# Gate and up projections as 2x2 block products with seven products, in a one-core decoder step

## What is computed

```
def rmsnorm(x, g, eps=RMS_EPS):
    xf = x.astype(jnp.float32)
    y = xf * lax.rsqrt(jnp.mean(xf * xf, axis=-1, keepdims=True) + eps)
    return (y * g.astype(jnp.float32)).astype(x.dtype)

def swiglu(h, w_gate, w_up, w_down):
    return (jax.nn.silu(h @ w_gate) * (h @ w_up)) @ w_down
...
# x += 0.5 * swiglu(rmsnorm(x)), D_MODEL = 1024, D_FF = 2816
# 512 prompt tokens and 64 sample tokens: T = 576 in all
```

## Time and profile before

| | us |
|---|---|
| median of three runs | 3361.85 (3356.53 to 3365.54) |
| the profiled execution, its own time | 3364.43 |
| its span, first to last instruction | 3362.6 |
| PE busy | 3111.3 (93%) |
| DVE busy | 1586.9 (47%) |
| ACT busy | 1170.0 (35%) |
| POOL busy | 424.7 (13%) |
| mean granted TensorE clock | 0.965 |

### The profile page before, as it was taken

The page is one execution under the profiler, slowest core; times in us unless marked ns, Lnnn a source line. Parts: engine busy times, 40 slices in busy tenths (PEclk is TensorE's granted clock), DMA queues, the critical chain, the costliest instruction groups (busy, mean ns, idle before and its releaser), DMA issues.

```text
span 3362.6 us, 70237 instructions
## 1 busy us (share of the span) xinstructions
PE 3111.3 (93%) x29771; PEld 2977.8 (89%) x29771; DVE 1586.9 (47%) x1892; ACT 1170.0 (35%) x1766; POOL 424.7 (13%) x352
## 2 busy tenths in 40 slices
PE   5999996999999988999999999798788997799999
PEld 5999996679999978999999999778788886799999
DVE  4333445556666654433444334444356654544333
ACT  3322223355555532322233222123344543233222
POOL 3000010220000003000020000400144433300000
PEclk9999998999999989999999999899899998899999
DMA  2222222011111102222222222311000001122222
GB/s 107 84 78 88 72 71 71 17 51 32 32 39 52 61 13 76 79 76 96 69 93 75 78 86 72 105 50 63 17 10 11 16 17 38 65 86 72 91 78 75
DMA packets 69248, 206.88 MB, mean 62 GB/s; under 512 B 25346, under 2 KB 42115, under 8 KB 53827
## 3 DMA queue, kind: packets, MB, share of 16 engines
q1 hardware_dynamic: 69058, 204.16, 18.3%
HBM read 198.63 MB, written 5.49 MB: 61 GB/s over the span
## 4 chain that ended last, share of the span: by engine, by line
PE 73%; DVE 6%; ACT 3%; issue 2%; POOL 1%; POOLq 0%; ACTq 0%; DVEq 0%
PE PS L233 45%; PE PS L1074 10%; PE PS L1706 6%; PE PS L1055 1%; PE PS L1101 1%; PE PS L1567 1%; DVE Y L2134 1%; PE PS L707 1%; PE PS L726 1%; PE PS L708 1%; PE PS L245 0%; PE PS L1078 0%; DVE MXP L1180 0%; DVE T L1626 0%; DVE XL L1636 0%
## 5 line engine op out<-in xcount | busy, mean ns | idle before, releaser
L233 PE MATMUL PS<-XH,WH 128*128 128x288 f32 x3520 | 759.2, 297 | 32.2 <-DVE XL L2374 17.7
L233 PE MATMUL PS<-XL,WH 128*128 128x288 f32 x3520 | 754.4, 296 | 0.0
L233 PE MATMUL PS<-XH,WL 128*128 128x288 f32 x3520 | 753.7, 296 | 0.0
L233 PEld LDWEIGHTS PS<-XH,WH 128*128 128x128 f32 x3520 | 569.7, 190 | 38.2 <-DVE WL L219 18.4
L233 PEld LDWEIGHTS PS<-XL,WH 128*128 128x128 f32 x3520 | 569.4, 190 | 0.0
L233 PEld LDWEIGHTS PS<-XH,WL 128*128 128x128 f32 x3520 | 569.1, 190 | 0.0
L219 DVE TENSOR_TENSOR WL<-RAW,WH 128x2048 fp32r<-128x2048 f32 (+1 forms) x184 | 421.6, 2292 | 286.6 <-ACT WH L214 285.7
L214 ACT ACTIVATE WH<-RAW 128x2048 fp32r<-128x2048 f32 (+1 forms) x185 | 344.4, 1862 | 388.4 <-PE PS L233 357.8
L329 ACT ACTIVATE T<-T 128x576 f32<-128x576 f32 x88 | 60.4, 686 | 706.6 <-DVE T L355 706.6
L233 PE MATMUL PS<-HH,WH 128*128 128x288 f32 x1408 | 300.8, 294 | 0.0
L233 PE MATMUL PS<-HH,WL 128*128 128x288 f32 x1408 | 300.0, 294 | 0.0
(11 more groups left out here) (483 smaller groups left out, 4387.0 us busy)
## 6 DMA issues: line engine op xcount, KB each, us to landing
RAW<-in_w SPq DMA_DIRECT2D x113, 1024.0 KB, 4.8
RAW<-in_w SPq DMA_DIRECT2D x32, 768.0 KB, 4.2
RAW<-in_w SPq DMA_DIRECT2D x32, 640.0 KB, 3.9
ROWS<-in_cache_c SPq DMA_DIRECT2D x128, 128.0 KB, 2.0
ROWS<-in_cache_kr SPq DMA_DIRECT2D x128, 32.0 KB, 1.8
RAW<-in_w SPq DMA_DIRECT2D x8, 384.0 KB, 3.2
X<-in_x SPq DMA_DIRECT2D x1, 2304.0 KB, 8.6
out_y<-X SPq DMA_DIRECT2D x1, 2304.0 KB, 6.9
```

Of the source, the lines that this page charges most:

```text
L233: mm = pe.matmul(PS[:, s, 2 * t + half, 0:HT], w[s][:, c:c + P], x[:, k, half * HT:(half + 1) * HT], start=(k == 0 and p == 0), stop=(k == ...
```

## The change

**Seven products.** In each FFN the first two gate-and-up items stay as they are. The other 20 are taken as a 2x2 block product: rows of blocks are gate and up, the inner index is the two halves of the 8 k tiles (k and k + 4), the columns are the two halves of the tokens. Winograd's form of Strassen's product makes of the eight block products seven, each of 4 k tiles x 3 = 12 matmuls of 288 columns: 84 matmuls instead of 96. It wants four sums of weight blocks for each item (S1 to S4, each 128 x 512), four sums of activations once for each FFN (t123_dve, t4_dve and their roundings), and sums of products behind PE.

**Who does what.** S1 is an addition on DVE; S3, S2 and S4 are three subtractions on POOL in a row, each from the one before it. ACT rounds the three own blocks and the four sums, DVE splits them. PE does the products in the order 5, 1, 7, 6, 2, 3, 4. Products 6, 3 and 4 are added onto banks that hold products 1, 5 and 7, so ACT first copies each of these aside (`keep_act` into `KEPT`), and PE waits for the copies. DVE adds up the four results, scales the gate half alone, and leaves the up half unscaled; 1/rms of the up half is put into `HALF` = 0.5/rms, by which down items are scaled.

**Parts and down items.** The 22 tiles are done in four parts of 4, 6, 6 and 6. A down item now holds two output tiles (d and d + 4), so that there are 4 for each part and 16 for each FFN as before, of 48 or 72 matmuls. They are evacuated by two DVE instructions of 1152 elements. The first down item leaves the last hidden row to the end.

**Around the FFN.** `norm_sums` moves behind the first item. Squares are taken on ACT in pairs, and POOL only adds them. FFN 2 and the latent projection take the k tiles in the order 0, 4, 1, 5, ... ACT's, DVE's, SP's and POOL's loops over an FFN are written out; PE keeps a loop over pairs of gate items. In the recurrence several semaphores are counted on one (`kk`, `y_norm`); its instructions stay the same.

```diff
-PARTS = (12, 10)
+PARTS = (4, 6, 6, 6)
...
+    def first_sum_dve(dve, n, js):
+        s = n % 2
+        dve.wait_ge(raw_in[s], 16 * (n // 2 + 1))
+        if n >= 2:
+            dve.wait_ge(multiplied, n - 1)
+        dve.tensor_tensor(sum_place(s, S1, "f"), RAW[s][:, 2 * QB:3 * QB], RAW[s][:, 3 * QB:4 * QB], ALU.add).then_inc(s1_ok, 1)
+
+    def sums_pool(pool, n, js):
+        s = n % 2
+        r = lambda b: RAW[s][:, b * QB:(b + 1) * QB]
+        pool.wait_ge(raw_in[s], 16 * (n // 2 + 1))
+        if n >= 2:
+            pool.wait_ge(multiplied, n - 1)
+        pool.tensor_tensor(sum_place(s, S3, "f"), r(0), r(2), ALU.subtract).then_inc(summed, 1)
+        pool.wait_ge(summed, 3 * js + 1)
+        pool.tensor_tensor(sum_place(s, S2, "f"), r(3), sum_place(s, S3, "f"), ALU.subtract).then_inc(summed, 1)
+        pool.wait_ge(summed, 3 * js + 2)
+        pool.tensor_tensor(sum_place(s, S4, "f"), r(1), sum_place(s, S2, "f"), ALU.subtract).then_inc(summed, 1)
...
+    def gate_pe(pe, n, i, j, ji, f, first=False):
...
+        pe.wait_ge(gate_lo, 5 * j + 3 + ji * 5)
+        pe.wait_ge(evacuated, n - 1 + CREDIT + i)
+        if first:
+            pe.wait_ge(t_split, 4 * f + 4)
+        whole(5).then_inc(part_mm, 1)
+        whole(1).then_inc(part_mm, 1)
+        pe.wait_ge(gate_lo, 5 * j + 4 + ji * 5)
+        whole(7).then_inc(part_mm, 1)
+        pe.wait_ge(gate_lo, 5 * j + 5 + ji * 5)
+        pe.wait_ge(kept, 3 * j + 2 + ji * 3)
+        whole(6, again=True).then_inc(part_mm, 1)
+        whole(2)
+        pe.wait_ge(item_split, n + 1 + i)
+        whole(3, again=True)
+        if first:
+            pe.wait_ge(t4_split, 4 * f + 4)
+        pe.wait_ge(e_ok, j + 1 + ji)
+        whole(4, again=True).then_inc(multiplied, 1)
...
+    def gate_dve(dve, n, js):
...
+        dve.wait_ge(multiplied, n + 1)
+        dve.wait_ge(kept, 3 * js + 3)
+        dve.tensor_tensor(T12[:, 0:HT], PS[:, s, 1, 0:HT], KEPT[:, 1, :], ALU.add)
+        dve.tensor_tensor(c12_21, PS[:, s, 2:4, 0:HT], u2, ALU.add)
+        dve.wait_ge(e_ok, js + 1)
+        dve.tensor_tensor(T12[:, 3 * HT:4 * HT], PS[:, s, 0, 0:HT], M57[:], ALU.add).then_inc(evacuated, 1)
+        dve.wait_ge(evacuated, n + 1 + CREDIT)
+        dve.tensor_tensor(T12[:, 0:T], T12[:, 0:T], RSTD[:], ALU.mult).then_inc(gate_scaled, 1)
...
+        for part, (n, cnt, j, _) in enumerate(hidden_steps(f)):
+            lone = 0
+            js = j - 2 * f - 2
+            if part == 0:
+                multiply_item(pe, n, 0, KD, 2, XH, XL, before=lambda k: pe.wait_ge(xhat_split, base + k + 1), order=order)
+                norm_sums(pe, norm, (n + 1) % 2)
+                pe.wait_ge(root, norm + 1)
+                multiply_item(pe, n + 1, 0, KD, 2, XH, XL)
+                gate_pe(pe, n + 2, 0, js + 2, 0, f, first=True)
+                gate_pe(pe, n + 3, 0, js + 3, 0, f)
+                lone = 4
...
+            for x in range(cnt):
+                plain = part == 0 and x < 2
+                more = x + 1 < cnt and not (part == 0 and x == 0)
                 if more:
-                    split_item(dve, n + u + 1, i)
...
+                    gate_own_act(act, n + x + 1)
+                else:
+                    round_item(act, n + x + 1, cols=ITEM if plain else 2 * cnt * P)
...
+                if not plain:
+                    keep_act(act, n + x, js + x, 0, first=part == 0 and x == 2)
+                if x:
+                    silu_act(act, j + x - 1)
+                if more:
+                    gate_sum_act(act, n + x + 1, js + x + 1, S1)
+                if not plain:
+                    keep_act(act, n + x, js + x, 1, first=part == 0 and x == 2)
+                if more:
+                    gate_sum_act(act, n + x + 1, js + x + 1, S3)
+                    gate_sum_act(act, n + x + 1, js + x + 1, S2)
+                if x:
+                    hidden_act(act, j + x - 1, x - 1)
+                if not plain:
+                    keep_act(act, n + x, js + x, 2, first=part == 0 and x == 2)
+                if more:
+                    gate_sum_act(act, n + x + 1, js + x + 1, S4)
...
+                if x:
+                    scaled(x - 1)
...
+                if more:
+                    first_sum_dve(dve, n + x + 1, js + x + 1)
+                    gate_own_dve(dve, n + x + 1, js + x + 1)
+                    gate_sum_dve(dve, n + x + 1, js + x + 1, S1)
...
+                if x:
+                    hidden_dve(dve, j + x - 1, n + x - 1, last_plain)
+                if not plain:
+                    rest_dve(dve, n + x, js + x)
+                if more:
+                    gate_sum_dve(dve, n + x + 1, js + x + 1, S3)
+                    gate_sum_dve(dve, n + x + 1, js + x + 1, S2)
+                if x:
+                    hidden_lo_dve(dve, j + x - 1, x - 1, last_plain)
+                if more:
+                    gate_sum_dve(dve, n + x + 1, js + x + 1, S4)
...
+                four = lambda t: t.rearrange("p o (a t) -> p o a t", a=2)
+                dve.tensor_tensor(four(DOWN[:]), PS[:, s, :, 0:HT].rearrange("p (o a) t -> p o a t", o=2),
+                                  halves(HALF[:]).unsqueeze(1).to_broadcast([P, 2, 2, HT]), ALU.mult).then_inc(down_ok, 1)
+                downs += 1
+                dve.wait_ge(down_ok, downs)
+                x = X[:].rearrange("p (o d) t -> p d o t", o=2)[:, d, :, :]
+                dve.tensor_tensor(x, DOWN[:], x, ALU.add).then_inc(evacuated, 1)
```

More of the change, by code:

```diff
@@ L50 @@
 ITEM = 16 * P
-N_FFN = sum(PARTS) + 2 * KD
+N_FFN = sum(PARTS) + 4 * len(PARTS)
 I_FFN0 = 0
@@ new lines, in gate_pe, with whole @@
+    def gate_pe(pe, n, i, j, ji, f, first=False):
+        s = n % 2
+        blocks = gate_blocks(s)
+        def whole(x, again=False):
+            b, w, v = blocks[x]
+            for k in range(4):
+                for p, (wp, xp) in enumerate(((0, 0), (0, 1), (1, 0))):
+                    mm = pe.matmul(PS[:, s, b, 0:HT], w[wp](k), v[xp](k), start=not again and k == 0 and p == 0,
+                                   stop=k == 3 and p == 2, skip_group_check=again)
+            return mm
+        pe.wait_ge(gate_lo, 5 * j + 3 + ji * 5)
[16 more added lines that the diff above has]
+        whole(4, again=True).then_inc(multiplied, 1)
@@ new lines, in keep_act, with rest_dve @@
+    def keep_act(act, n, js, x, first=False):
+        act.wait_ge(part_mm, 4 * js + (0, 1, 3)[x] + 1)
+        if js and x == 0:
+            act.wait_ge(e_ok, js)
+        if js and x:
+            act.wait_ge(evacuated, n + CREDIT - (1 if first else 0))
+        act.activation(KEPT[:, x, :], PS[:, n % 2, (2, 0, 0)[x], 0:HT], ACT.Copy).then_inc(kept, 1)
+    def rest_dve(dve, n, js):
+        dve.wait_ge(part_mm, 4 * js + 3)
+        dve.wait_ge(kept, 3 * js + 1)
+        dve.tensor_tensor(M57[:], PS[:, n % 2, 3, 0:HT], KEPT[:, 0, :], ALU.add).then_inc(e_ok, 1)
@@ L298, in ffn_sp, with ffn_pe @@
     def ffn_sp(sp, f):
[L299 to L303, removed]
+        for n, cnt, _, row in hidden_steps(f):
+            load_items(sp, n, cnt, 16, peel=2 if n == 0 else 0, row=row)
+            load_downs(sp, n + cnt, cnt, row + cnt)
+    def ffn_pe(pe, f, order=None):
         norm = NORM_OF_FFN[f]
         base = 8 * XHAT_OF_NORM[norm]
[L306 to L343, removed]
@@ new lines, in ffn_pool @@
+    def ffn_pool(pool, f, norm=None):
+        steps = list(hidden_steps(f))
+        for part, (n, cnt, j, _) in enumerate(steps):
+            js = j - 2 * f - 2
+            for x in range(cnt):
+                if x + 1 < cnt and not (part == 0 and x == 0):
+                    sums_pool(pool, n + x + 1, js + x + 1)
+            d0 = n + cnt
+            if part + 1 < len(steps):
+                sums_pool(pool, d0 + 4, js + cnt)
+            elif norm is not None:
+                zero_squares(pool, norm)
+                for d in range(4):
+                    sq_pair_pool(pool, norm, d)
```

539 lines of the change are left out of this document (384 added, 155 removed), and 2 rows, old and new, of the table q.

## The result

The changed kernel takes 3399.2 us (median of 6, 3392.2 to 3406.8), the kernel before 3368.4 beside it (3356.5 to 3377.0): a ratio of 1.0096, with a 95% interval of 1.0071 to 1.0121. The forecast was 3330 with a range of 3240 to 3380: the time lies outside it, and on the other side of the kernel before. The profiled execution took 3396.55 us with a span of 3394.7, 32.1 longer than before.

What follows compares the result with a forecast made beforehand. PE was taken as the bound, FFN time being its number of matmuls. 20.9 us gained inside the FFNs plus 11.5 around them, 32.4 off 3364.4, gave 3332, as a median 3330, range 3240 to 3380.

Steps and rivals of the forecast that it cites:

- Matmuls removed: In the four FFNs, 20 items each lose 12 matmuls: 960 at 0.1322 us, 126.9 us saved.
- The turns: In middle items, DVE's two-input SBUF work and POOL's subtractions exclude each other; PE loses 1.35 us an item, 16.2 an FFN.
- the schedule: One item's engine work timed from PE's end of the item before: copy of product 1 at 6.05, item 12.4 us.
- Handovers: Losses at the parts' first items, 1.95 us three times an FFN, and in part 1, 4.45 us an FFN.
- the net of +20.9: Inside the FFNs: 126.9 us from removed matmuls less 106 us lost, 20.9 us gained.
- Around the FFNs: Between FFNs and at their starts, shorter waits gain 19.6 us and 8.1 is given back: net 11.5 us gained.
- The author's estimate for the same three subtractions on DVE: With POOL's subtractions on DVE, an item takes DVE 9.8 + 3 x 0.69 = 11.9 us, making DVE the bound.
- the scaling did not get in first: Rival inside items: DVE's scaling beats POOL's S2, losing 0.2 us an item, 40 in place of 106; 3264 us, chance 0.25.
- The turns exist: Rival inside items: no turns for these subtractions, only handovers remain, some 5 us an FFN; 3243 us, chance 0.08.
- The clock did not fall in the items: Rival inside items: stalls halve PE's clock, 1.7 us more each; 3432 us, or 3381 if half of them do; chance 0.13.
- The term of 3.4 us at half clock: In the clock rival, a gap of 1.35 to 1.95 us halves PE's clock for 3.4 us, costing 1.7 more.
- The last sign that was named: A gap ahead of product 5 or 3, for DVE's splits, would mean DVE has more work in an item than counted.

Runs made afterwards that it cites:

- e10: The changed kernel with POOL's three weight-block subtractions of each item moved to DVE, between S1's sum and the own blocks, ACT's order unchanged: 3271.9 us.
- e1: The changed kernel with ACT's copy of product 1 moved right behind product 5's, ahead of Silu and S1's rounding: 3296.1 us.
- e7: The changed kernel without the seven products: all 22 gate-and-up items of 96 matmuls, no weight or activation sums: 3365.5 us, against 3364.7 for the kernel before.
- e3: The changed kernel with ACT's root of the norm moved ahead of its four roundings of activation sums: 3384.9 us.
- e6: The changed kernel with the copy of product 1 first on ACT and POOL's three subtractions of each item moved to DVE: 3268.1 us.

## Why the prediction was wrong, step by step

**Matmuls removed, 126.9:** right, 28811 instead of 29771, 0.1322 us each where they run unbroken.

**The turns:** right in mechanism. S2 keeps the scaling waiting, S4 goes ahead of the S1 sum; the copy was put at 6.05 us behind the end of the item, and ends at 1571.93, 6.1 behind the readings' start at 1565.86. The loss for an item was put at 1.35 and is 1.68. The term is mis-sized by small things: DVE's readings start 0.2 us behind PE's first matmul of the item (1565.66), where the schedule had 0.1; the chain from there to the copy's end is 6.1 long, not 5.95; and PE loses 0.15 more than the copy is late. Over 48 middle items the 0.33 us make 16. e10 shows the turns as a cause: without them 22.4 of the 135.3 us are left. e1 shows the copy's place as one too: 33.4 are left.

**Handovers:** the first items of parts 3 and 4 lose 1.1, not 1.95. In part 1 it is the other way. Item 2 was put at 1.2 and loses 2.5 to 4.1. Behind the part of four tiles 1.6 was put, and PE stood for 3.84 and then went on at half clock (0.50). The schedule had one item's sums there. The rows show POOL at two items' in a row, beside DVE's splits:

```profile
1408.13 3.99 DVE L405 TENSOR_TENSOR WL<-RAW,WH 128x1024 fp32r<-128x1024 f32 x2
1412.05 1.74 DVE L414 TENSOR_TENSOR WSL<-WSF,WSH 128x512 fp32r<-128x512 f32 x1
...
1410.22 1.35 POOL L378 TENSOR_TENSOR WLF<-RAW 128x512 f32<-128x512 f32 x1 [0.86 <-PE PS L279]
1411.65 1.59 POOL L380 TENSOR_TENSOR WSF<-RAW,WLF 128x512 f32<-128x512 f32 x1
```

The same pair of splits (1024 and 512 elements) takes 1.82 where POOL is quiet, and the split of 512 elements 0.68. In the FFNs altogether: 135.3 where 106 was forecast, so the net of +20.9 gained became 8.4 lost. This alone moves the sum by 29 us.

**Around the FFNs:** the step that failed. "Item 1 waits for the root, ACT's roundings of the next item to 1.7, a table load of 1.28 and the root's 0.75 ...: 2.5 of idling" left out what stands ahead of the root in ACT's program, the four roundings of activation sums, and that they wait for DVE's 16 token sums. The forecast had these sums only ahead of item 2, and only in FFN 0 (2.2 us); elsewhere it gave DVE's backlog 0.4. The wait was 12.1 us in FFN 0, 9.2 in FFN 1, 10.7 in FFN 2 and 5.6 in FFN 3, each followed by a stretch at half clock (0.50 for 3.7 to 5.6 us), in which item 1 took 14.6 to 15.4 us instead of 12.7. In FFN 0 item 1 was put at 41.9 and started at 51.9. e7, without the sums, has the forecast's size, 3.1. e3 shows the order on ACT as the first half of it and DVE's work as the second, and e6 that POOL's part in it is small. The 11.5 gained became 23.7 lost: 35 us, of which the waits beyond 2.5 are some 28. The gain of 11.5 was perhaps itself too high: e7, which has all of it but the token sums, gains 4 there in its one trace.

**The author's estimate for the same three subtractions on DVE, with DVE as the bound:** wrong in the bound, and short in the gain. It added 3 x 0.69 to the forecast's 9.8, so 11.9 us of DVE for an item where the forecast for the change had items of 12.4, and put the time about 30 us under the forecast's sum; the rows of e10 show 10.45, since neighbours overlap at their ends (0.76 every 0.67), and items come 11.1 us apart. It gives some 3300; e10 took 3271.9. The gain over the change is 127 us, 113 of it in the FFNs, at the handovers too.

**The rivals:** the scaling did not get in first: S2 won by 0.03 us, not 0.2, but in all 48 middle items of the trace. The turns exist. The clock did not fall in the items: it is 1.00 in 1533.64:1584.76 with a stall of 1.4 us in each item, so slower came by another road than the one given for it. The term of 3.4 us at half clock fits the one gap of the earlier trace rows with a fall behind it (0.79 over 8 us is 3.4 us at 0.50). The half clock was paid behind the long waits. Where PE stood for 3.84 us, once in each FFN, the clock was 0.50 for 3.4 to 5.7 us behind it; the window behind the gap in FFN 1:

```profile
1413.00:1418.00 5.00, 4.08 (x17) 4.08 (x18) 4.97 (x6) 0.41 (x1) 1.84 (x2) 0.50 0.06 13
```

The last sign that was named, a gap ahead of product 5 for splits on DVE, is there only behind the part of four tiles.

## What to carry to other kernels

Before an instruction with two SBUF inputs goes on GpSimd, look at what DVE does in that stretch: a subtraction of 1.3 us there cost DVE 1.1 us each time they met, and DVE did the same in 0.69. In a queue in program order, walk the whole list ahead of the one instruction that PE waits for, with what each of them waits for, and put copies and roots that PE wants ahead of those that can wait: one moved line (e1) was worth 103 us. The root's move (e3) was worth 14, because DVE's work was the next thing waited for. And an engine that is called full by a sum of single durations may still have room: measure it.

## What the runs showed that was not expected

- Whether a stall lowers PE's clock is not a matter of its length alone in these rows. Idle gaps of 1.40 us once an item never did: behind all 48 the granted clock was 1.00. Of gaps of 2.26 us in the same kernel, those at 72.2 and 1799.59 were followed by half clock (0.50 for 3.4 us), those at 1363.48 and 2994.85 were not (1.00). Those of 3.84 were, in all four FFNs.
- A DVE instruction of 0.76 us beside a POOL instruction that reads SBUF took 1.87, one of 0.68 took 1.78. Each ended 0.5 to 0.6 us behind the end of POOL's, though by its plain length 0.7 remained: its start seems to run beside the end of the other's. Which part overlaps, no run here tells.
- DVE's instructions with a duration of 0.76 us start 0.67 apart in a row, so a sum of durations overstates DVE: 11.7 us for the 17 instructions of an item of e10, where the window shows 10.45.
